# A two-block transformer kernel: the output gate products of the second block placed between the steps of its two attentions

## The chip, the cores and the metric

The kernel runs on one core of a Trainium2 chip, as one program. The metric is the device time of one execution in microseconds (us). The engines are TensorE (PE, with its weight loads as PEld), VectorE (DVE), ScalarE (ACT), GpSimd (POOL) and SyncE (SP), which issues most of the DMAs. Each engine goes through its own list of instructions in order and waits on semaphores.

## What is computed

The input x has 512 tokens of width 1024. A first block (differential attention, sparse attention with compressed keys, merge, MLP) and a second block follow. The change is in the second block, which in the reference is, shortened:

```python
def second_block(x, ...):
    h = x
    # layer 0: FOX
    u = rmsnorm(h, norm_a_g)
    q, k, v, f_logit, gate = split(u @ w_in_a)      # 1024, 1024, 1024, 16, 1024 columns
    q = rmsnorm(q per head); k = rmsnorm(k per head)
    log_f = log_sigmoid(f_logit + b_forget)
    o = fox_attention(q, k, v, log_f)               # 16 heads of 64, causal, with decay c_q - c_k
    h = h + (o * silu(gate)) @ w_out_a
    # layer 1: SWA
    u_kv = rmsnorm(h, kv_norm_g)
    k_s, v_s = split(u_kv @ w_kv)                   # 4 key heads; k normed, partly rotated
    u = rmsnorm(h, norm_b_g)
    q, gate = split(u @ w_in_b)                     # 1024, 1024; q normed, partly rotated
    o = swa_sink_attention(q, k_s, v_s, sinks)      # 16 query heads, window of 128, a sink logit
    h = h + (o * silu(gate)) @ w_out_b
    return h
```

## The kernel before

The program is one list for each engine, built by nested Python functions. All matrix products are made of three passes with numbers split in a high and a low part (high x high, high x low, low x high), in fp32r.

`plan()` gives an ordered table of product groups in runs. A group makes 512 output columns from 1024 rows. Its weights come in units of 512 x 512 numbers (1 MB): SP loads a unit into one of two slots of `RAW` (`weights`, issued at L352), ACT makes the high part in `SPL` (`split_hi`, L488 with a norm gain as scale, L494 without), DVE the low part (`split_lo`, L779 with the gain, L787 without), and PE multiplies (`unit` and `product`, L1421), into four of the eight PSUM banks, alternately for even and odd groups. A unit is split while PE works on the one before. `evict` copies a finished group out of PSUM: into `QKV` (L528), through Silu into `MX` (L532), or onto the residual `X`. Normed groups then go through POOL (squares L1331, rotation L1340) and DVE (`norm_one`, `norm_two`, L828 to L861) with a square root on ACT (L549).

The run `fox_in` has the gate columns first (`fgate0`, `fgate1`: 192 matmuls), then the narrow forget gate `fg`, queries, keys and values; the forget gate's sums over time are made by small chains on DVE (`forget`, `decay_sums`) and stored in DRAM. The run `swa_in` has keys and values (`skv`), queries (`sq0`, `sq1`) and, last, the gate columns (`sgate0`, `sgate1`: 192 matmuls). The attention follows, then the output run (`fox_out`, `swa_out`), for FOX with the next layer's norm behind it.

`attend` is one function for all four attentions. A unit is a pair of heads, there are eight units in FOX and in SWA, and a unit has four steps, one for each tile of 128 queries, from the last tile (t = 3) to the first; in FOX a step has (t+1) x 128 keys, in SWA at most 256. `over_units` runs the first three units and the last three steps written out and those between in a loop with registers. SP copies the unit's query and key columns from `QKV` to a stage (`stage_units`, L371), the values (L386) and in FOX the decays (L379). PE turns queries and keys (`turn`, L1712), ACT and DVE make the high and low parts in `QKT` (L633, L1008). PE makes the scores (`scores_of`: L1649, decays L1655, band L1658, causal mask L1659), DVE the negative maximum (L978, in SWA after it placed the sink, L975), ACT the exponentials with their sums (L614) in `PB`, DVE the reciprocal (L983), POOL scales P (L1369), PE turns P (`turn_p`, L1678), ACT and DVE copy a head each (L625, L1003), and PE makes the values (`values_of`, L1698), for a key tile j at once over all the queries that see it, so 128 to 512 columns, and head 0 and head 1 into different halves of the partitions. In FOX and SWA, DVE then multiplies the output of the unit by the finished gate (L1026), ACT and DVE split the result into `HT` (`high` L638, `low` L1032), which the output product reads. The P of one unit is turned while the scores of the next are made:

```python
if scores: scores_of(m, 3)
if last:   values_of(b.before(), 0)
if values: turn_p(b, 3)
```

`X` (the residual) and `Y` share one region of SBUF; `PB` shares the region of `SPL`, so that weights of the output run can be split only after the attention (`hold=` in `run`). After FOX come the angles for the rotation in SWA (`angles` on DVE, a sine on ACT, L763), before the output run.

## Time and profile before

| | us |
|---|---|
| median of 3 runs | 1947.2 (1944.85 to 1955.84) |
| the profiled execution: its own time | 1947.98 |
| its span from first to last instruction | 1946.2 |
| PE busy | 1759.8 (90%) |
| DVE busy | 892.9 (46%) |
| ACT busy | 705.7 (36%) |
| POOL busy | 366.0 (19%) |

Mean granted TensorE clock over the span: 0.940 of 2.4 GHz. DMA moved 154.85 MB, 80 GB/s in the mean.

How to read it: times are of one execution. A PE matmul's end is modelled, so "busy" says that PE had matmuls under way, not that it was at its peak. The second block lies between about 1294 us and the end: FOX between 1485.8 and 1612.87, SWA between 1786.1 and 1892.67.

### The profile page before, as it was taken

How to read it: one execution, taken by the hardware profiler on the slowest of the kernel's cores; microseconds unless marked ns; L12 is line 12 of the kernel's file. 1: busy time of each engine (PE TensorE's matmuls, PEld its weight loads, DVE VectorE, ACT ScalarE, POOL GpSimd, SP SyncE). 2: the span in 40 equal slices, each digit the busy share in tenths (PEclk: the TensorE clock that was granted, in tenths of full speed). 3: DMA queues.
4: the chain of work that ended last, by engine and by line, in shares of the span. 5: the costliest groups of instructions: out<-in, count | busy, mean ns of one | idle time of the engine just before them, and what ended most of it. 6: DMA issues, size and time to landing. Idle time of an engine off the chain costs nothing.

```text
span 1946.2 us, 24116 instructions
## 1 busy us (share of the span) xinstructions
PE 1759.8 (90%) x8846; PEld 1348.3 (69%) x8846; DVE 892.9 (46%) x1569; ACT 705.7 (36%) x1525; POOL 366.0 (19%) x490
## 2 busy tenths in 40 slices
PE   2999888999978998997999999989998998798878
PEld 2888656887664554886888888868775546686547
DVE  2485274224544665344342234231662653353661
ACT  3322365122135666323341233132323552433550
POOL 4251042102213655010000000000111440020320
PEclk9999797999987999999999999989998998898899
DMA  5223222323102221432223232322222112132211
GB/s 128 85 87 122 73 76 65 108 87 108 44 12 52 58 67 30 153 108 87 66 89 105 88 107 87 108 65 86 87 82 71 55 34 88 64 108 68 63 41 68
DMA packets 148049, 154.85 MB, mean 80 GB/s; under 512 B 48972, under 2 KB 90172, under 8 KB 147960
## 3 DMA queue, kind: packets, MB, share of 16 engines
q1 hardware_dynamic: 141768, 152.74, 24.8%
q0 software_dynamic: 992, 0.86, 0.3%
q10 hardware_dynamic: 5200, 0.02, 0.3%
q8 instruction: 61, 1.00, 0.2%
q14 instruction: 28, 0.23, 0.0%
HBM read 123.15 MB, written 2.15 MB: 64 GB/s over the span
## 4 chain that ended last, share of the span: by engine, by line
PE 83%; DVE 7%; ACT 6%; issue 3%; ACTq 1%; POOL 0%; DVEq 0%; POOLq 0%
PE ps L1421 61%; PE ps L1649 4%; PE ps L1678 3%; PE ps L1698 3%; PE ps L1712 2%; ACT pb L614 2%; PE ps L1659 2%; DVE qkt L1008 1%; ACTq L476 1%; DVE nm L978 1%; ACT qkt L633 1%; PE ps L1655 1%; PE ps L1549 1%; PE ps L1519 1%; PE ps L1620 1%
## 5 line engine op out<-in xcount | busy, mean ns | idle before, releaser
L1421 PE MATMUL ps<-spl,ht 128*128 128x512 f32 x2496 | 583.0, 396 | 31.5 <-DVE spl L787 16.3
L1421 PEld LDWEIGHTS ps<-spl,ht 128*128 128x128 f32 x2496 | 477.8, 192 | 135.0 <-issue 13.6
L787 DVE TENSOR_TENSOR spl<-raw,spl 128x1024 fp32r<-128x1024 f32 x196 | 253.5, 1336 | 568.5 <-ACT spl L494 568.5
L494 ACT ACTIVATE spl<-raw 128x1024 fp32r<-128x1024 f32 x196 | 196.3, 1052 | 640.0 <-PE ps L1421 639.1
L1421 PE MATMUL ps<-ht,spl 128*128 128x512 f32 x1536 | 351.8, 391 | 2.0 <-DVE spl L787 2.0
L1421 PEld LDWEIGHTS ps<-ht,spl 128*128 128x128 f32 x1536 | 289.9, 189 | 63.2 <-issue 2.9
L614 ACT ACTIVATE pb<-ps,nm 128x512 f32<-128x512 f32 (+5 forms) x320 | 161.4, 513 | 85.9 <-DVE nm L978 85.9
L978 DVE TENSOR_REDUCE nm<-ps 128x1 f32<-128x512 f32 (+5 forms) x320 | 140.0, 467 | 81.9 <-PE ps L1659 78.7
L1421 PE MATMUL ps<-spl,uu 128*128 128x512 f32 x768 | 174.4, 389 | 0.0
L1421 PEld LDWEIGHTS ps<-spl,uu 128*128 128x128 f32 x768 | 144.1, 188 | 29.9
L1649 PE MATMUL ps<-qkt 64*128 64x256 f32 (+2 forms) x960 | 126.4, 372 | 15.8 <-issue 7.0
L1331 POOL TENSOR_TENSOR sq<-qkv 128x2048 f32<-128x2048 f32 (+1 forms) x15 | 51.5, 3435 | 451.2 <-ACT qkv L528 436.6
L1678 PEld LDWEIGHTS ps<-idf,pb 128*128 128x128 f32 x672 | 74.9, 144 | 62.4 <-issue 51.2
L1369 POOL TENSOR_TENSOR pb<-pb,rr 128x256 f32<-128x256 f32 (+3 forms) x128 | 81.5, 660 | 191.3 <-DVE rr L983 191.2
L1649 PEld LDWEIGHTS ps<-qkt 64*128 64x128 f32 x960 | 80.0, 208 | 49.5 <-issue 40.8
L1369 POOL TENSOR_TENSOR pb<-pb,rg 128x512 f32<-128x512 f32 (+3 forms) x160 | 112.8, 721 | 7.5
L1698 PE MATMUL ps<-pt,stv 128*64 128x256 f32 (+3 forms) x512 | 94.1, 446 | 20.3 <-ACT pt L625 11.0
L1678 PE MATMUL ps<-idf,pb 128*128 128x128 f32 x672 | 109.9, 289 | 0.0
L625 ACT ACTIVATE pt<-ps 128x256 f32<-128x256 f32 (+3 forms) x160 | 67.8, 424 | 86.5 <-PE ps L1678 86.1
L1008 DVE TENSOR_TENSOR qkt<-ps,qkt 128x512 fp32r<-128x512 f32 x80 | 54.9, 686 | 94.6 <-ACT qkt L633 94.6
L1421 PE MATMUL ps<-ys,spl 128*128 128x512 f32 x384 | 88.9, 394 | 0.0
L1379 POOL MEMSET nws<- 128x2048 f32 x2 | 3.6, 1807 | 440.0 <-PE ps L1421 440.0
(244 smaller groups left out, 1562.8 us busy)
## 6 DMA issues: line engine op xcount, KB each, us to landing
raw<-w_in SPq DMA_DIRECT2D x30, 1024.0 KB, 5.2
raw<-w_mlp_up SPq DMA_DIRECT2D x16, 1024.0 KB, 5.2
raw<-w_mlp_down SPq DMA_DIRECT2D x16, 1024.0 KB, 5.1
raw<-w_in_a SPq DMA_DIRECT2D x16, 1024.0 KB, 5.3
stq<-qkv SPq DMA_DIRECT2D x56, 256.0 KB, 2.7
raw<-w_in_b SPq DMA_DIRECT2D x8, 1024.0 KB, 5.1
stq<-qkv SPq DMA_DIRECT2D x48, 128.0 KB, 2.5
raw<-w_proj_diff SPq DMA_DIRECT2D x4, 1024.0 KB, 5.1
```

The source lines that it names most:

```text
L494: act.activation(SPL[:, n % 2, HI, 2 * k:2 * k + 2], RAW[:, n % 2, 2 * k:2 * k + 2], ACT.Copy).then_inc(hi_done, 1)
L614: last = act.activation(p, PS[:, 2 * (idx % 2) + h, 0:w], ACT.Exp, bias=NM[:, m.slot, h, t:t + 1], accum_out=LS[:, m.slot, h, t:t + 1])
L625: act.activation(PT[odd][:, 0 if a.is_diff else idx % 2, 0:w], PS[:, 4 + odd, 0:w], ACT.Copy)\
L787: dve.tensor_tensor(SPL[:, n % 2, LO, 2 * k:2 * k + 2], RAW[:, n % 2, 2 * k:2 * k + 2], SPL[:, n % 2, HI, 2 * k:2 * k + 2].bitcast(F32), A ...
L978: dve.tensor_reduce(top, bank[:, 0:w + a.sink], AX.X, ALU.max, negate=True).then_inc(s["mx"], 1)
L1008: dve.tensor_tensor(QKT[:, m.slot, i, LO], PS[:, 7], QKT[:, m.slot, i, HI].bitcast(F32), ALU.subtract)\
L1331: pool.tensor_tensor(SQ[:, :, 0:w], QKV[:, :, col:col + w], QKV[:, :, col:col + w], ALU.mult)\
L1369: last = pool.tensor_tensor(p, p, by[:, m.slot, h, t:t + 1].to_broadcast([P, w]), ALU.mult)
L1421: last = pe.matmul(PS[:, b0 + b], left[:, x], right[:, y], start=(kt == 0 and i == 0), stop=(kt == UK * g["units"] - 1 and i == 2))
L1649: pe.matmul(PS[:, 2 * (idx % 2) + h, 0:w], QKT[r, m.slot, 0, x, P * t:P * t + P], QKT[r, m.slot, 1, y, P * a.first_key(t):P * t + P], star ...
L1678: last = pe.transpose(bank[:, P * i:P * i + P], PB[:, m.slot, h, o:o + P], IDF[:])
L1698: last = pe.matmul(PS[HD * h:HD * h + HD, 6, cols], STV[:, m.slot, j, v], PT[h][:, idx % 2, 0:w], start=(idx == 0 and not (a.is_nsa and m. ...
```

## The change

The gate groups leave `fox_in` and `swa_in`. They become a "side" group of eight tiles (128 gate columns each, 24 matmuls), whose weights come in four units of 256 columns x 1024 rows. A tile's 24 matmuls are cut in five pieces (6, 6, 3, 6, 3) that PE does between the steps of a unit of attention. In FOX one tile (`lead=1`) is made before the first scores, in SWA two. The tile is copied raw into `MX` by ACT (`keep_tile`), and Silu comes for all eight tiles at the end of the attention.

The attentions FOX and SWA get a function of their own, `attend_beside`, fully written out (64 steps in all, no loop). Queries, keys and values are read in place from `QKV` (no staging); in SWA keys are turned once for two units. P is kept in three buffers of one step each (`PBS`), in FOX in the region of `X`; so the residual is stored in DRAM during `fox_in` (`XD`) and loaded again after the last P was turned. P is turned one step after its scores, and its values made one step after that; the values are made for each query tile by blocks of 128 x 128. A finished unit's output is copied over its own query columns; the multiplication by the gate and the split (`gated`, `gated_hi`) follow for all eight after the attention. Weights of the side units and of the first two output units are split during the attention, in halves (`side_hi`, `side_lo`), so the output run starts with split weights. The angles move beside the output products. The core of the diff:

```diff
+        [("fq0", ...), ("fg", ...narrow...), ("fq1", ...)] + fk0, fk1, fv0, fv1
+    runs["fox_side"] = [("fgate", "w_in_a_2", FGATE, 0, 4, "side", "ht", ("side",))]
...
-        + [(f"sgate{i}", "w_in_b_2", D + W * i, 0, 2, "col", "ht", ("act", "Silu", "mx", i)) for i in range(2)])
+    runs["swa_side"] = [("sgate", "w_in_b_2", D, 0, 4, "side", "ht", ("side",))]
...
+FOX = Attention("fox", 8, lead=1, run="fox_side")
+SWA = Attention("swa", 8, banded=True, lead=2, run="swa_side")
+EARLY, LATE = 0, 1
+SIDE_KTS = {(0, LATE): (0, 2), (1, EARLY): (2, 4), (1, LATE): (4, 5), (2, EARLY): (5, 7), (2, LATE): (7, 8)}
+PT_BANK, PV_BANK, SIDE_BANK = 0, 2, 3
...
 SP:
+            weights(RUNS["fox_in"], only=4)
+            sp.wait_ge(freed["dve"], RUNS["mlp"][-1]["freed"])
+            sp.dma_start(XD, X[:].rearrange("p t n -> p (t n)")).then_inc(x_parked, 16)
+            weights(RUNS["fox_in"], skip=4)
...
+            side_weights(FOX, 0)
+            sp.wait_ge(cum_out, 16)
+            sp.wait_ge(n_done, RUNS["fox_in"][4]["normed"] + 1)
+            decays(0)
+            decays(1)
+            side_weights(FOX, 1)
+            side_weights(FOX, 2)
+            side_weights(FOX, 3)
+            decays(2)
+            decays(3)
+            weights(RUNS["fox_out"], only=1)
+            decays(4)
+            weights(RUNS["fox_out"], skip=1, only=1)
+            for m in range(5, FOX.units):
+                decays(m)
+            sp.wait_ge(*need(FOX, "pt_tr", FOX.steps))
+            sp.dma_start(X[:].rearrange("p t n -> p (t n)"), XD).then_inc(x_back, 16)
...
 ACT, attend_beside:
+                for n in range(a.steps + 2):
+                    m, i = divmod(n, NT)
+                    if n + 1 < a.steps:
+                        exps(n + 1)
+                    if i == 1 and m:
+                        keep(m - 1)
+                    if i == 0 and m + 1 < a.units and a.new_keys(m + 1):
+                        high(m + 1, 1)
+                    if i == 3 and a.tile_at(m) is not None:
+                        keep_tile(a.tile_at(m))
+                    if 1 <= n <= a.steps:
+                        turned(n - 1)
+                    if n >= a.steps:
+                        silu(2 * (n - a.steps))
+                        silu(2 * (n - a.steps) + 1)
+                    if i == 3 and m + 2 < a.units:
+                        high(m + 2, 0)
+                    if i in (0, 2):
+                        split(m, i // 2)
+                for k in range(4, KT):
+                    silu(k)
...
 DVE, attend_beside:
+                for n in range(a.steps + 1):
+                    m, i = divmod(n, NT)
+                    if n + 1 < a.steps:
+                        maxima(n + 1)
+                    if i == 0 and m + 1 < a.units and a.new_keys(m + 1):
+                        low(m + 1, 1)
+                    if i in (0, 2):
+                        split(m, i // 2)
+                    if n >= 1:
+                        turned(n - 1)
+                    if n + 1 < a.steps:
+                        norms(n + 1)
+                    if i == 3 and m + 2 < a.units:
+                        low(m + 2, 0)
...
 PE, attend_beside:
+                def part(m, i, when):
+                    if a.tile_at(m) is None or (i, when) not in SIDE_KTS:
+                        return
+                    first, end = SIDE_KTS[i, when]
+                    if first == 0:
+                        pe.wait_ge(*need(a, "kept", a.tile_at(m)))
+                        pe.wait_ge(*need(a, "qt", min(m + 2, a.units)))
+                        pe.wait_ge(*need(a, "kt", a.keys_of(min(m + 1, a.units - 1)) + 1))
+                    side(a.tile_at(m), first, end)
...
+                for n in range(a.steps + 2):
+                    m, i = divmod(n, NT)
+                    if n + 1 < a.steps:
+                        scores_of(n + 1)
+                    if n >= 2:
+                        values_of(n - 2)
+                    if i == 0 and m + 1 < a.units and a.new_keys(m + 1):
+                        pe.wait_ge(*need(a, "qt", m + 2))
+                        pe.wait_ge(*need(a, "kept", min(m + a.lead, SIDE_TILES)))
...
+                        turn(m + 1, 1)
+                    part(m, i, EARLY)
+                    if 1 <= n <= a.steps:
+                        turn_p(n - 1)
+                    part(m, i, LATE)
+                    if i == 3 and m + 2 < a.units:
+                        pe.wait_ge(*need(a, "kept", min(m + a.lead + 1, SIDE_TILES)))
+                        turn(m + 2, 0)
```

POOL's `attend_beside` scales the P of a step when its reciprocal is there, as before. `split(m, part)` does half a weight unit in every other unit of attention (units 1, 3, 5, 7 in FOX; 0, 2, 4, 6 in SWA). The lists of ACT and DVE at the end:

```diff
-            attend(FOX)
-            ...sines...
-            run(RUNS["fox_out"], hold=[(A["fox"]["pt_tr"], 4 * FOX.units), (y_lo, 3 * KT)], follow=True, norm=3)
-            run(RUNS["swa_in"], primed=True)
-            attend(SWA)
+            attend_beside(FOX)
+            run(RUNS["fox_out"], primed=True, follow=True, first=lambda: gated_hi(FOX), at={1: sines}, norm=3)
+            run(RUNS["swa_in"], primed=True, follow=True)
+            attend_beside(SWA)
+            run(RUNS["swa_out"], primed=True, first=lambda: gated_hi(SWA))
```

## Rows read from the trace of the kernel before

**Rows 1.** Windows: stage, length, then busy us (count) per engine, granted clock, DMA.
```profile
core 0: us, PE busy (x) PEld busy (x) DVE busy (x) ACT busy (x) POOL busy (x), PEclk, DMA share, GB/s
1485.80:1612.87 127.07, 109.75 (x673) 60.14 (x673) 72.86 (x175) 67.35 (x191) 47.11 (x64) 0.88 0.16 47
1530.00:1542.60 12.60, 12.57 (x88) 6.94 (x84) 8.60 (x20) 7.68 (x24) 6.00 (x8) 1.00 0.22 64
1786.10:1892.67 106.57, 78.55 (x608) 49.65 (x609) 66.16 (x226) 60.29 (x192) 34.41 (x64) 0.88 0.19 45
1838.50:1849.20 10.70, 8.74 (x77) 5.49 (x76) 7.95 (x28) 6.71 (x23) 4.24 (x9) 1.00 0.25 63
```

**Rows 2.** PE's timeline (start, us, what) at the attentions' starts.
```profile
1482.78 0.84 PE L1421 MATMUL ps<-spl,ht 128*128 128x512 f32 x3
...
1742.37 43.68 PE L1421 MATMUL ps<-ht,spl 128*128 128x512 f32 x192
```

**Rows 3.** Windows of PE alone: length, busy us, granted clock, DMA.
```profile
1414.00:1421.00 7.00, 5.28 (x13) 0.52 0.46 150
1503.00:1516.00 13.00, 12.20 (x51) 0.50 0.18 49
1892.67:1899.00 6.33, 6.33 (x16) 0.54 0.64 236
```

**Rows 4.** Waits of PE after 1320 us: us in total, times, longest.
```profile
PE ps L1421 <- DVE cum L1124: 4.3, 1, 4.3
PE ps L1421 <- ACT fl L541: 1.9, 1, 1.9
```

**Rows 5.** Timeline of all engines within a steady FOX unit.
```profile
1532.51 0.96 PE L1649 MATMUL ps<-qkt 64*128 64x512 f32 x6
...
1534.36 1.08 PE L1698 MATMUL ps<-pt,stv 128*64 128x512 f32 x4
...
1535.37 0.44 PE L1678 MATMUL ps<-idf,pb 128*128 128x128 f32 x2
...
1535.96 0.20 ACT L614 ACTIVATION_READ_ACCUMULATOR pb<-ps,nm 128x1 f32 x1
...
1537.36 0.44 PE L1698 MATMUL ps<-pt,stv 128*64 128x128 f32 x4
1537.73 0.66 PE L1678 MATMUL ps<-idf,pb 128*128 128x128 f32 x4
...
1540.17 0.60 ACT L633 ACTIVATE qkt<-ps 128x512 fp32r<-128x512 f32 x1 [0.24 <-PE ps L1712]
...
1540.80 0.69 DVE L1008 TENSOR_TENSOR qkt<-ps,qkt 128x512 fp32r<-128x512 f32 x1 [0.30 <-ACT qkt L633]
```

**Rows 6.** Groups by shape in the two attentions' windows: busy us, mean ns, idle before.
```profile
L494 ACT ACTIVATE spl<-raw 128x1024 fp32r<-128x1024 f32 x3 | 2.9, 1040 | 0.0
L787 DVE TENSOR_TENSOR spl<-raw,spl 128x1024 fp32r<-128x1024 f32 x2 | 2.4, 1222 | 1.4 <-ACT spl L494 1.4
L532 ACT ACTIVATE mx<-ps 128x512 f32<-128x512 f32 x4 | 2.1, 602 | 15.8 <-PE ps L1421 15.8
```

**Rows 7.** Timeline of all engines within a steady SWA unit.
```profile
1837.66 0.62 PE L1649 MATMUL ps<-qkt 64*128 64x256 f32 x6 [0.53 <-DVE qkt L1008]
...
1840.20 0.19 ACT L614 ACTIVATION_READ_ACCUMULATOR pb<-ps,nm 128x1 f32 x1
```

**Rows 8.** Timeline of ACT and DVE beside the products of sq1.
```profile
1723.35 2.03 ACT L528 ACTIVATE qkv<-ps 128x512 f32<-128x512 f32 x4
...
1731.76 2.56 ACT L488 ACTIVATE spl<-raw,lng 128x512 fp32r<-128x512 f32 x4
...
1740.62 0.69 DVE L861 TENSOR_TENSOR qkv<-qkv,sq 128x512 f32<-128x512 f32 x1
```

**Rows 9.** Timeline between FOX's last values and the first output product.
```profile
1606.74 1.28 ACT L763 ACT_TABLE_LOAD   x1
...
1612.87 1.19 PE L1421 MATMUL ps<-spl,ht 128*128 128x512 f32 x2 [7.54 <-DVE spl L787]
```

**Rows 10.** DMA issues: count, KB each, median us to landing.
```profile
x_res<-x SPq DMA_DIRECT2D x1, 2048.0 KB, 7.7
```

More of the change, by code:

```diff
@@ L110, in plan @@
                 tables.append(then[3])
-            out[name].append(dict(by=by, freed=freed[by], name=n, weight=w, col=c, row=r, units=units, kind=kind, src=src, then=then,
+            out[name].append(dict(by=by, freed=freed.get(by), name=n, weight=w, col=c, row=r, units=units, kind=kind, src=src, then=then,
                                   unit=unit, group=group, normed=normed, rotated=rotated, turned=turned,
@@ L151, in __init__ @@
         self.is_diff, self.is_nsa, self.is_fox, self.is_swa = (name == x for x in ("diff", "nsa", "fox", "swa"))
+        self.lead, self.run, self.steps = lead, run, NT * units
     def first_key(self, t):
@@ L318, in program, with score_bank, turn_bank, first_bank @@
         NEXT_GROUP = [RUNS[r][0]["group"] for r in ("diff_in", "mlp", "fox_in", "swa_in")]
+        SIDE = {a.name: RUNS[a.run][0] for a in (FOX, SWA)}
+        TURNS = {a.name: a.turns() for a in (FOX, SWA)}
+        def score_bank(a, s, h):
+            return 4 * (1 - SIDE[a.name]["group"] % 2) + 2 * (s % 2) + h
+        def turn_bank(a, n):
+            return 4 * (SIDE[a.name]["group"] % 2) + n
+        PT_BANK, PV_BANK, SIDE_BANK = 0, 2, 3
+        def first_bank(m, i):
+            return SIDE_BANK if (m, i) not in ((0, 0), (0, 1), (1, 0)) else 2 * m + i
+        def wide(x):
+            return x.rearrange("p k (b n) -> p (k b) n", n=SIDE_W)
+        def kept_output(m):
+            return QKV[:, :, P * m:P * m + P]
+        def by_tile(x):
+            return x.rearrange("p (t n) -> p t n", n=P)
         def reach(eng, s, value):
@@ L342, in weights @@
             def weights(groups, skip=0, only=None):
-                units = [(g, u) for g in groups for u in range(g["units"])][skip:only]
+                units = [(g, u) for g in groups for u in range(g["units"])][skip:][:only]
                 for g, u in units:
@@ L643, in step @@
                         exps(m, 3)
-                    if last and (a.is_fox or a.is_swa):
-                        high(b.before())
                     if values:
@@ L668, in narrow_hi, with gated_hi @@
+            def gated_hi(a):
+                s, base = A[a.name], 2 * KT if a.is_fox else 3 * KT
+                g = SIDE[a.name]
+                act.wait_ge(unit_used, g["unit"] + g["units"])
+                for k in range(KT):
+                    act.wait_ge(*need(a, "gated", k + 1))
+                    act.activation(HT[:, HI, k], MX[:, k], ACT.Copy).then_inc(y_hi, 1)
             def narrow_hi(i, n):
@@ L767, in _, with sines @@
-            attend(SWA)
-            run(RUNS["swa_out"], hold=[(A["swa"]["pt_tr"], 4 * SWA.units), (y_lo, 4 * KT)])
+            run(RUNS["fox_in"], primed=True, follow=True, at={0: lambda: narrow_hi(1, 16), 3: forget})
+            attend_beside(FOX)
+            def sines():
+                act.wait_ge(p_link, N_ANGLE)
+                act.activation(ANG[:, 2], ANG[:, 0], ACT.Sin)
+                act.activation(ANG[:, 3], ANG[:, 1], ACT.Sin).then_inc(small_act, 1)
+            run(RUNS["fox_out"], primed=True, follow=True, first=lambda: gated_hi(FOX), at={1: sines}, norm=3)
@@ L1050, in step @@
                         difference(b, 0)
-                    if last and (a.is_fox or a.is_swa):
-                        low(b.before())
                     if scores:
@@ L1350, in attend @@
                 s = A[a.name]
-                by = RG if a.is_diff or a.is_nsa else RR
                 def unit(m):
@@ L1374, in attend, with attend_beside @@
                     unit(Unit(2 * i + 1, 1, i))
+            def attend_beside(a):
+                s = A[a.name]
+                for n in range(a.steps):
+                    m, i = divmod(n, NT)
+                    t = NT - 1 - i
+                    w = a.width(t)
+                    pool.wait_ge(*need(a, "r", n + 1))
+                    for h in range(2):
+                        p = PBS[a.name][n % 3][:, h, 0:w]
+                        last = pool.tensor_tensor(p, p, RR[:, m % 2, h, t:t + 1].to_broadcast([P, w]), ALU.mult)
+                    last.then_inc(s["scaled"], 1)
             def clear_narrow(last):
@@ L1449, in bank_free @@
                     for o in r:
-                        if o["group"] == g["group"] - 2:
+                        if o["group"] == g["group"] - 2 and o["kind"] != "side":
                             pe.wait_ge(freed[o["by"]], o["freed"])
+                for a in (FOX, SWA):
+                    s, side = A[a.name], SIDE[a.name]["group"]
+                    if g["group"] == side + 1:
+                        pe.wait_ge(*need(a, "e", a.steps))
+                    if g["group"] == side + 2:
+                        pe.wait_ge(*need(a, "pt_a", a.steps))
+                        pe.wait_ge(*need(a, "pt_b", a.steps))
+                        pe.wait_ge(*need(a, "o", a.units))
+                        pe.wait_ge(*need(a, "kept", SIDE_TILES))
             def narrow(g, i):
```

411 lines of the change are left out of this document (314 added, 97 removed).

## Prediction

> **What bounds the kernel now.** I read the windows of the two stages that the change rebuilds, then their timelines, then the waits. The first attention of the second block (FOX) takes 127.07 us, the second (SWA) 106.57 us; a FOX unit of 12.60 us holds 12.57 us of TensorE work, a SWA unit of 10.70 us holds 8.74 us [rows 1]. So the middle of FOX is bound by TensorE, and SWA leaves 2 us free per unit; the rest of the free time lies at the ends. The gate products run as a dense block of 192 matmuls in 43.68 us ahead of SWA, and an equal block ahead of FOX [rows 2]. The stages to compare are, before: FOX from the last projection product (1483.62) to the first output product (1612.87), 129.3 us, plus 43.7 = 173.0; SWA from the end of the query products (1742.4) to 1892.67 = 150.3, its gates included. FOX starts after a pause of TensorE, and the granted clock is then 0.50 (the 1.2 GHz level) until about 1516 [rows 3], over two units. That is the largest thing the change can win.
>
> **The work that moves.** A gate tile is 24 matmuls, 5.46 us [rows 2]; it moves, it doesn't vanish. Value products change their cut. One with 512 columns takes 1.01 us (1534.36 to 1535.37), one with 128 columns 0.37 (1537.36 to 1537.73) [rows 5]: 0.16 fixed and 0.213 per 128 columns. After, each 128x128 block is its own product with its own weight load. I count 0.05 once and 0.32 per block: ten blocks in four groups 3.4 us against 2.77, +0.63 per FOX unit; seven blocks in SWA, +0.33. Bounds: a gain of nothing, and ten times 0.37, +0.93. The Trainium skill (TensorE: Matmul & The Clock Gate, Engine queue depths) says that the queue pulls weight loads ahead of running matmuls; by that the finer cut would be free and the kernel 8 us faster than my sum. The 0.16 fixed part of the rows speaks for the loads being paid. A FOX unit is then 12.57 + 0.63 + 5.46 = 18.7 us of TensorE, a SWA pair with one key turn fewer 28.9 us.
>
> **The waits that the new order adds.** ACT and DVE go through their lists in order. I walk a unit by the code of the diff with the durations of the rows; time 0 is the start of the 512-column scores that stand in a unit's fourth step.
> FOX, fourth step: scores 1.85 (1532.51 to 1534.36), values 1.01, turning P 0.59 (the row's 0.66 less its drain) [rows 5]: TensorE is at the query turn at 3.45. That turn uses the gate tile's bank, and the tile's copy stands in ACT's list behind both exponentials, which end 3.65 after the scores began (1532.51 to 1536.16) [rows 5]. With 0.6 for the copy the turn starts at 4.35: a wait of 0.9. Next unit, first step: scores at 4.95, values, key turn and P turn end at 8.2. The gate piece after them writes the bank from which the keys are split, so it waits for ACT's high part (behind the exponentials, which end at 8.2) and DVE's low part, 0.60 and 0.69 [rows 5]: 9.65, a wait of 1.4. Steps two and three have none. Period 18.7 + 2.3 = 21.0 us.
> In every other unit a weight unit is split in halves, 1.04 us on ACT and 1.22 on DVE [rows 6]. In step three ACT has its half behind its copy of the turned P, DVE has its half ahead of its own copy. Values and the next maxima wait for both: +1.65 us per such unit.
> FOX in all: start 7.4 (three turns and one dense tile, beside which ACT and DVE get ready), unit 0 17.2, six units at 21.0, three splits 5.0, from there to the last P turn 21.0. Then a new tail: copy 0.3, table load 1.28 [rows 9], eight Silu at 0.52 [rows 6], the last output's copy 0.6, high 0.63, low 0.69, in all 8.1. TensorE idles 7.5 us in it, as it does today at that place (7.54) [rows 9]. Sum 184.7 against 173.0: **+11.7**. That the clock stays at 1.00 at FOX's start, dense work leading in, is within this sum.
> SWA, two units: exponentials end 2.73 after the scores began (1837.66 to 1840.39) [rows 7]. By the same walk the query turns wait 1.3 and 1.4, and the key's copies hold the gate piece 1.9. In the even unit the split half of step one holds DVE's copy of P: exponentials 7.35, copy 7.6, high half 1.5, low half 1.6, copy 0.3, so 11.2, and TensorE wants it at 8.2: 3.0. The half of step three costs 2.5. Waits 10.1, pair 39.0 us; two units and two tiles are 32.3 today. The 1.5 lies between 1.28 by elements and 2.56 by count (four instructions of half the width of the 2.56) [rows 8]; most of such a duration goes with the elements in rows 6. The pair that splits output weights, without scale: 37.5.
> SWA's start: the norm of the last query half is no longer hidden by the gate block. For the first half it took 18.0 us from ACT's copy (1723.35) to the last add (1741.31) [rows 8], 2.1 the copy and 14.9 of the rest its own steps. After, ACT first splits a side unit (3.0), so it ends at 20.0. ACT's root waits in it until 11.6, so tile 0 is copied at 14.0 only, and TensorE is idle from 7.5 to 14.1. The clock then falls: after today's last such pause 6.33 us of dense work ran at 0.54 [rows 3], 3 us lost. Scores start at 22.7. Unit 0 12.1, unit 1 20.7, pairs 39.0 and 37.5, two last units 28.0, tail 8.1: 168.1 against 150.3: **+17.8**.
> At nothing: the residual parked in DRAM. Out, some 30 us pass before a weight unit behind it is wanted; back, 23 us of output products run before it is read. 2 MB landed in 7.7 us [rows 10], which is the cost without that cover. The staging copies of Q, K and V vanish, 56 by the code; SP had time for them. The angles move beside output products. The forget gate's two waits, 1.9 and 4.3 us [rows 4], keep their distance. In SP's list the decay loads wait for scores, and the weights behind them are wanted a unit or more later; each staging step it drops stood nowhere on the path.
> Sum: 1947.98 + 11.7 + 17.8 = 1977.5, against the profiled execution (1947.98, span 1946.2), which is 0.8 above the median of 1947.2; **1976.5** on the median. Some 30 waits good to 0.3 us each, and value blocks from -8 to +4, give 1962 to 1992.
> The Trainium skill (ScalarE: Activation LUTs, What ACT_TABLE_LOAD costs) adds a drain of 1.38 us to a switch of tables; by that the two tails are 2.8 us longer. The row shows 1.28 and the next work behind it at once where that was ready, and the sum goes by it.
>
> **Rivals.** **A, TensorE stays the bound** and the waits don't come up. FOX: eight units of 13.2 and eight tiles 149.3, tail 7.5, last chain 3: 159.8, 13 less than today. SWA: four pairs 115.6, the start's pause with its clock 11, last chain 3, tail 7.5: 137.1, 13 less. Steps at the ends that nothing fills give back 7: 1928 (1921 to 1936). For it: a deeper order (P is turned two steps after its scores, three buffers for P), ACT 7.68 and DVE 8.60 of 12.60 us busy [rows 1]. Against it: the waits come from the order in the lists, not from load. It decides if the copies end before TensorE asks, 1.4 us earlier in FOX. 0.18.
> **B, half the waits**, where exponentials end earlier than in my walk. The waits outside start and tail are 16 and 8 us in FOX and 32 in SWA; half is 28, 1948.5 (1941 to 1958). 0.14.
> **C, the clock falls inside SWA.** One pause of 4.3 us [rows 4] put 5.28 us of work to half clock [rows 3], 2.6 us and more. The waits of 3.0 and 2.5 us come eight times; if the clock falls after six of them for 3.5 us, it is 21 more: 1998. Against it: the wait of 1.9 us passed at full clock. 0.07. The Trainium skill (TensorE: Matmul & The Clock Gate, Why this matters for your kernels) warns of idle gaps between bursts; no row here shows one of this size within an attention.
>
> **How the numbers follow.** The main case has 0.61, A 0.18, B 0.14, C 0.07. About 0.5% (9.7 us) is what a measurement of this kernel can tell from no change. The main case and C are slower whole, B is no change but for 0.02 on the slower side, A is faster. So 0.18, 0.12 and 0.70. The range leaves out the lower half of A and the upper half of C: 1930 to 1995; the slower cases alone have 1958 to 1995.
>
> **What would show it.** Right: FOX units near 21 us, SWA pairs near 39; TensorE idle before turns and before the first gate piece of a unit, for copies of ACT and DVE; clock 1.00 at FOX's start; a pause of 6 us in SWA's first 15 us; 7 us idle ahead of each output product. Wrong: FOX units under 19.5 us with TensorE busy over 95%, value blocks at 0.2 us each, or the return of the residual ending a wait.

## The result, and the profile after

The changed kernel takes 2016.8 us in the median of four runs (2014.14 to 2018.71); the kernel before takes 1948.97 beside it. The ratio is 1.0343, with a 95% interval of 1.0309 to 1.0378: 68 us slower. The forecast was 1976.5 with a range of 1930 to 1995: the direction was right, the slowdown more than twice as large as the sum said, and the time outside the range. The profiled execution spans 2017.1 us, 70.9 more than before's, at a mean granted clock of 0.92 (before 0.94).

The two stretches that the prediction compares, in the windows view (length, PE busy, granted clock, DMA share, GB/s), of the changed kernel:

```profile
1443.20:1642.60 199.40, 165.67 (x1058) 0.85 0.08 29
1771.70:1963.90 192.20, 151.06 (x914) 0.78 0.09 30
```

FOX with its gates takes 199.4 us against 173.0 before and 184.7 in the forecast; SWA 192.2 against 150.3 and 168.1. Together they are 68.3 of the 70.9 us. The units answer to [rows 1] (after the length: PE, PEld, DVE, ACT and POOL busy, clock, DMA share, GB/s):

```profile
1520.76:1541.73 20.97, 18.38 (x133) 12.57 (x133) 7.86 (x18) 9.14 (x26) 5.59 (x8) 1.00 0.00 1
1541.73:1565.29 23.56, 19.95 (x133) 13.57 (x133) 8.85 (x21) 8.97 (x25) 5.59 (x8) 0.93 0.13 46
1840.00:1886.90 46.90, 39.51 (x231) 26.47 (x230) 16.74 (x59) 17.39 (x55) 8.61 (x17) 0.75 0.06 23
```

The first is a FOX unit at full clock: 20.97 us, where the walk gave 21.0. The next unit has the same 133 matmuls and takes 2.6 more, at a mean clock of 0.93. The third is a SWA pair, 46.9 us at 0.75, where the walk gave 39.0. So a unit can come out as the walk has it, to a tenth of a microsecond, but most were lengthened by something that the walk left out. The waits of PE (us in total, times, longest), after 1320 us:

```profile
PE ps L2095 <- DVE pts L1309: 26.3, 17, 3.3
PE ps L2119 <- DVE qkt L1314: 15.4, 10, 3.1
PE ps L1713 <- DVE ht L1346: 13.2, 2, 6.6
PE ps L2105 <- ACT mx L810: 11.4, 11, 1.3
PE ps L2119 <- ACT mx L810: 5.1, 1, 5.1
```

L2095 are the values, L2119 the gate pieces, L2105 the turns, L1713 the output products. These are the kinds of wait that the walk has. PE's timeline over one FOX unit and the start of the next, cut to four of the waits, with the same kind of gate piece twice:

```profile
1530.29 1.60 PE L2119 MATMUL ps<-ht,spl 128*128 128x512 f32 x6 [1.65 <-DVE qkt L1314]
1531.83 0.62 PE L2057 MATMUL ps<-qkt 64*128 64x256 f32 x6
...
1544.46 0.88 PE L2095 MATMUL ps<-pts,qkv 128*64 128x128 f32 x12 [0.80 <-DVE pts L1309]
...
1547.06 0.66 PE L2105 MATMUL ps<-idf,qkv 128*128 128x128 f32 x4 [1.14 <-ACT mx L810]
...
1552.36 2.90 PE L2119 MATMUL ps<-ht,spl 128*128 128x512 f32 x6 [1.68 <-DVE qkt L1314]
1555.19 0.82 PE L2057 MATMUL ps<-qkt 64*128 64x256 f32 x6
```

The six matmuls of the gate piece took 1.60 us at 1530.29 and 2.90 at 1552.36. The second time PE had waited 0.80 and 1.14 us shortly before, besides the 1.68 just ahead: the clock had fallen to its lower level (1.2 GHz) after three short pauses and came back after the piece. In SWA's first four units the values wait longer, 2.6 to 2.9 us each time. The cause of one such wait, on DVE:

```profile
1811.17 1.67 DVE L985 SCALAR_TENSOR_TENSOR spl<-raw,lng,spl 128x256 fp32r<-128x256 f32 x4 [5.53 <-ACT spl L579]
1812.76 0.42 DVE L1309 COPY pts<-ps 128x256 f32<-128x256 f32 x1
```

DVE had idled 5.53 us for ACT's high half of a weight unit, whose split stands in its list ahead of the copy of the turned P; PE's values (1813.32) wait for that copy. It is the order in the lists, not load: DVE is busy 36% of the FOX stretch and 41% of SWA's.

### The profile page after: what moved, and what is told of

The parts are those of the page before. It is cut to its first block, busy times and chain, and to the rows that moved or that the text cites. A ratio compares the mean times of both kernels' runs of the same rounds, so it can differ in the third digit from the quotient of the medians.

```text
span 2017.1 us, 24292 instructions
## 1 busy us (share of the span) xinstructions
PE 1803.0 (89%) x9150; PEld 1385.2 (69%) x9150; DVE 892.0 (44%) x1581; ACT 722.0 (36%) x1568; POOL 362.2 (18%) x490
## 3 DMA queue, kind: packets, MB, share of 16 engines
q1 hardware_dynamic: 116584, 145.40, 22.7%
## 4 chain that ended last, share of the span: by engine, by line
PE 79%; ACT 9%; DVE 7%; issue 3%; ACTq 1%; POOL 0%; DVEq 0%; POOLq 0%
PE ps L1713 54%; PE ps L2119 5%; PE ps L1948 2%; PE ps L2095 2%; PE ps L1972 2%; ACT pb L725 2%; PE ps L2077 2%; PE ps L2057 1%; ACTq L568 1%; PE ps L1991 1%; PE ps L2005 1%; DVE qkt L1229 1%; DVE nm L1199 1%; ACT qkt L744 1%; PE ps L1953 1%
## 5 line engine op out<-in xcount | busy, mean ns | idle before, releaser
L1713 PE MATMUL ps<-spl,ht 128*128 128x512 f32 x2496 | 584.3, 397 | 31.8 <-DVE ht L1346 13.2
L1713 PEld LDWEIGHTS ps<-spl,ht 128*128 128x128 f32 x2496 | 478.7, 192 | 135.0 <-issue 13.9
L1010 DVE TENSOR_TENSOR spl<-raw,spl 128x1024 fp32r<-128x1024 f32 x180 | 234.8, 1347 | 524.1 <-ACT spl L605 524.1
L1713 PE MATMUL ps<-ht,spl 128*128 128x512 f32 x1152 | 263.9, 391 | 2.0 <-DVE spl L1010 2.0
L1713 PEld LDWEIGHTS ps<-ht,spl 128*128 128x128 f32 x1152 | 217.6, 189 | 48.1 <-issue 2.9
L1713 PE MATMUL ps<-spl,uu 128*128 128x512 f32 x768 | 174.4, 389 | 0.0
L1713 PEld LDWEIGHTS ps<-spl,uu 128*128 128x128 f32 x768 | 144.2, 188 | 29.9
L2119 PE MATMUL ps<-ht,spl 128*128 128x512 f32 x384 | 122.8, 460 | 20.4 <-DVE qkt L1314 15.4
L725 ACT ACTIVATE pb<-ps,nm 128x512 f32<-128x512 f32 (+1 forms) x192 | 99.8, 530 | 45.7 <-DVE nm L1199 45.6
L1199 DVE TENSOR_REDUCE nm<-ps 128x1 f32<-128x512 f32 (+1 forms) x192 | 85.3, 486 | 54.6 <-PE ps L1953 54.4
L2119 PEld LDWEIGHTS ps<-ht,spl 128*128 128x128 f32 x384 | 77.9, 218 | 41.9 <-issue 22.8
L1713 PE MATMUL ps<-ys,spl 128*128 128x512 f32 x384 | 90.1, 397 | 0.0
L1921 PE MATMUL ps<-idf,xn 128*128 128x128 f32 x128 | 30.8, 421 | 61.2 <-DVE xn L1181 61.2
L1713 PEld LDWEIGHTS ps<-ys,spl 128*128 128x128 f32 x384 | 73.9, 193 | 15.9 <-issue 0.2
L1948 PE MATMUL ps<-qkt 64*128 64x384 f32 (+3 forms) x576 | 77.5, 377 | 7.3 <-DVE qkt L1229 3.0
L2095 PE MATMUL ps<-pts,qkv 128*64 128x128 f32 x544 | 53.5, 329 | 29.2 <-DVE pts L1309 26.3
L1665 POOL TENSOR_TENSOR pbf<-pbf,rr 128x512 f32<-128x512 f32 (+3 forms) x64 | 44.7, 720 | 185.5 <-DVE rr L1303 185.5
L1296 DVE TENSOR_REDUCE nm<-ps 128x1 f32<-128x257 f32 (+5 forms) x128 | 54.5, 439 | 37.5 <-PE ps L2067 34.8
```

The source lines that it names most:

```text
L725: last = act.activation(p, PS[:, 2 * (idx % 2) + h, 0:w], ACT.Exp, bias=NM[:, m.slot, h, t:t + 1], accum_out=LS[:, m.slot, h, t:t + 1])
L1010: dve.tensor_tensor(SPL[:, n % 2, LO, 2 * k:2 * k + 2], RAW[:, n % 2, 2 * k:2 * k + 2], SPL[:, n % 2, HI, 2 * k:2 * k + 2].bitcast(F32), A ...
L1199: dve.tensor_reduce(top, bank[:, 0:w], AX.X, ALU.max, negate=True).then_inc(s["mx"], 1)
L1296: dve.tensor_reduce(NM[:, m % 2, h, t:t + 1], bank[:, 0:w + a.sink], AX.X, ALU.max, negate=True)\
L1665: last = pool.tensor_tensor(p, p, RR[:, m % 2, h, t:t + 1].to_broadcast([P, w]), ALU.mult)
L1713: last = pe.matmul(PS[:, b0 + b], left[:, x], right[:, y], start=(kt == 0 and i == 0), stop=(kt == UK * g["units"] - 1 and i == 2))
```

## The experiments

Each kernel is built from the changed one; the parts are combined as the text says. All but the last version are single timed runs. The kernel before took 1949.88 beside e1 to e5, 1947.1 beside the runs whose label begins with f, 1950.2 beside g1 and g2. In these traces FOX starts between 1436.6 and 1443.4 us, though none of the edits touches what stands ahead of it; a single time can differ by as much without a cause in the edit, so the stretches are the safer comparison.

**DVE copies first.** DVE copies the turned P and takes the reciprocals ahead of its half of a weight split:

```diff
+                    if n >= 1:
+                        turned(n - 1)
+                    if n + 1 < a.steps:
+                        norms(n + 1)
                     if i in (0, 2):
                         split(m, i // 2)
-                    if n >= 1:
-                        turned(n - 1)
-                    if n + 1 < a.steps:
-                        norms(n + 1)
```

> One edit: DVE copies the turned P and makes the reciprocal before its half of a weight split, not after. Theory (order of the lists): the waits of the value products on DVE's copies, 26 us in the trace of the changed kernel (0.8 to 3.4 us each, 14 of them), go down to a few us, and as they are the longest pauses of TensorE the granted clock of the SWA units rises from 0.72 to 0.77 towards 1.00: 2016.8 - 20 - 10 = 1987 us. Rival 1 (the waits cost only their own length): 1997 us, with the clock of the units as it was. Rival 2 (the clock falls for another reason and the waits only move to the next copy): over 2010 us.

Measured: 1997.95 us. PE's waits:

```profile
PE ps L2105 <- ACT mx L810: 19.0, 12, 3.2
PE ps L2119 <- DVE qkt L1314: 14.2, 10, 3.1
...
PE ps L2095 <- ACT pts L791: 10.9, 8, 3.1
```

The 26.3 us for DVE's copy fall to 3.5, but 7.6 come back in the wait for the gate tile's copy on ACT (11.4 to 19.0) and 8.0 in the one for ACT's own copy of P: the next late engine. One wait of a chain taken away gives what the next in the chain leaves. The number is that of rival 1, its picture is not: the waits in the attentions shrank by 8.5 us in all, and the clock did change. In FOX it stayed low (0.84, units of 24.4 us, a stretch of 195.3 us), in SWA it rose from 0.78 to 0.88 and the stretch fell from 192.2 to 174.4.

**All three orders.** In addition ACT copies the gate tile ahead of the exponentials of step four, and the gate pieces start in a unit's second step, where they need not wait for the keys' copies:

```diff
-SIDE_KTS = {(0, LATE): (0, 2), (1, EARLY): (2, 4), (1, LATE): (4, 5), (2, EARLY): (5, 7), (2, LATE): (7, 8)}
+SIDE_KTS = {(1, EARLY): (0, 3), (1, LATE): (3, 4), (2, EARLY): (4, 6), (2, LATE): (6, 8)}
...
+                    if i == 3 and a.tile_at(m) is not None:
+                        keep_tile(a.tile_at(m))
                     if n + 1 < a.steps:
                         exps(n + 1)
```

> The edit of the run before, and two more: ACT copies the finished gate tile before the exponentials of the next step, and the first gate piece of a unit moves from the first step to the second (pieces of 9, 3, 6, 6 matmuls). Theory: beside the 26 us the waits at the query turns (14 us) and at the first gate piece (15 us) go, and the clock stays up: FOX units near 19.0 us, SWA pairs near 32 us, 2016.8 - 55 - 12 = 1950 us. Rival 1 (waits by their length alone): 1962 us. Rival 2 (TensorE's own work has grown by the pieces): FOX units over 20.5 us with TensorE over 97% busy, 1975 us or more.

Measured: 1952.06 us, 65 less than the changed kernel, with every matmul of it. Windows of PE (the two stretches, a FOX unit, a SWA unit with a key turn) and waits:

```profile
1441.30:1603.10 161.80, 145.59 (x1057) 0.97 0.11 36
1732.30:1897.30 165.00, 137.59 (x914) 0.85 0.11 35
1484.72:1503.25 18.53, 18.01 (x134) 1.00 0.19 58
1771.94:1794.00 22.06, 20.56 (x122) 0.77 0.15 49
```

```profile
PE ps L1713 <- DVE ht L1346: 13.4, 2, 6.8
PE ps L2095 <- ACT pts L791: 12.1, 11, 3.1
...
PE ps L2095 <- DVE pts L1309: 7.6, 13, 1.0
```

The six inner FOX units are now 18.5 us each, TensorE busy 97% of them, and FOX is 11.2 us shorter than before the change (161.8 against 173.0). SWA, at 165.0 against 150.3, loses 14.7. Its pair of units takes 37.7 us, not the 32 expected, and its clock is still low (0.85), though between unit 0 and the last two no wait is over 1.2 us. This is PE in the unit of 22.06 us, where the key turn (L2108, L2109) goes over to the low clock:

```profile
1773.83 0.66 PE L2095 MATMUL ps<-pts,qkv 128*64 128x128 f32 x8 [0.94 <-ACT pts L791]
1775.04 0.30 PE L2108 MATMUL ps<-idf,qkv 128*64 128x128 f32 x1 [0.56 <-DVE qkt L1314]
1775.27 0.43 PE L2109 MATMUL ps<-idf,qkv 128*64 128x128 f32 x2
1775.63 0.42 PE L2108 MATMUL ps<-idf,qkv 128*64 128x128 f32 x1
1775.98 0.69 PE L2109 MATMUL ps<-idf,qkv 128*64 128x128 f32 x2
```

Pauses of 0.94 and 0.56 us are the only ones in the nine us ahead of this fall.

**Two of the three.** Without the order on DVE:

> The changed kernel with two of the three list edits: ACT copies the gate tile ahead of the exponentials, and the gate pieces start in a unit's second step; DVE's split stays ahead of its copy of the turned P. If the three edits add up (the first alone gave 19, all three 65): 2016.8 - 46 = 1971. If what counts is how many pauses follow one another, then FOX, with 0.8 us left in every other unit, keeps 1.00 and its units are 18.6 and 19.4 us, and SWA, where DVE's waits of 2.6 us stay, still falls to half clock: FOX as in the run with all three (161.8 us stretch) plus 4 x 0.8, SWA 165 + 8 waits of 2.0 more + clock 6: 1952 + 3 + 22 = 1977. If DVE's order is what brings the clock down, the time is 1985 or more.

Measured: 1976.41 us. The number is that of the second theory, but by two errors that cancel: FOX is 178.1 us, where that theory has 165, and SWA 171.5, where it has 187. In FOX the wait of 0.8 us grew to 2.18 once the others no longer hid it, the units with a split took 20.2 to 22.8 us instead of 19.4, and the clock fell in two of the three. Each of them has this one pause and no other over 0.3 us within 20 us of it, so pauses need not follow one another for the clock to fall:

```profile
1477.21 0.70 PE L2095 MATMUL ps<-pts,qkv 128*64 128x128 f32 x4 [2.18 <-DVE pts L1309]
1477.84 4.21 PE L2119 MATMUL ps<-ht,spl 128*128 128x512 f32 x9
```

The first order alone is worth 19 us, the other two 40, all three 65.

**Pauses filled.** The waits stay, and TensorE does useless work in them. Its products are added into the bank of the unit's output, so this kernel serves for its times alone:

```diff
+                def fill(m, i, where):
+                    if a.tile_at(m) is None:
+                        return
+                    for _ in range(FILL.get((a.name, m % 2, i, where), 0) if m or i == 3 else 0):
+                        pe.matmul(PS[:, turn_bank(a, PV_BANK)], HT[:, HI, 0, 0:P], HT[:, HI, 1], start=False, stop=False,
+                                  skip_group_check=True)
```

> The changed kernel, with matmuls of no use (128 x 512, the residual's first tile by its second, added into the bank of the unit's output, which is therefore wrong) put where TensorE waits in the trace of the changed kernel: FOX 4 before the query turn, 6 before the first gate piece, 3 before the values of step four in the units with a split; SWA 4, 4, and 10 before the values that wait 2.6 us. At 0.23 us each they take about as long as the waits, so that no other engine is served later than before. Theory (the pauses of 0.8 to 2.9 us, coming close together, put TensorE to the 1.2 GHz level, and this costs what my sum lacks): the granted clock is 1.00 in FOX from its second unit on and nearly so in SWA, the stretches at half clock inside the attentions (about 78 us in the changed kernel, in which six gate matmuls took 2.90 instead of 1.60 us) vanish, and the kernel takes 2016.8 - 30 = 1987 us (1980 to 1995), though TensorE does more work. Rival (the order of the lists alone makes the units long, the clock falls with the small matmuls and transposes and not with the pauses): the low stretches stay where they are and the time is 2017 or more.

Measured: 1991.38 us. The windows of PE (FOX and SWA stretch, then one FOX unit with a split) and its timeline in that unit:

```profile
1442.80:1630.90 188.10, 169.58 (x1127) 0.93 0.09 31
1760.80:1937.10 176.30, 150.96 (x1008) 0.92 0.10 33
1532.98:1555.04 22.06, 21.51 (x147) 1.00 0.13 49
```

```profile
1534.71 0.94 PE L2139 MATMUL ps<-ht 128*128 128x512 f32 x3
1535.70 0.88 PE L2096 MATMUL ps<-pts,qkv 128*64 128x128 f32 x12
...
1536.92 1.17 PE L2139 MATMUL ps<-ht 128*128 128x512 f32 x4
1538.30 0.66 PE L2106 MATMUL ps<-idf,qkv 128*128 128x128 f32 x4 [0.21 <-ACT mx L811]
```

L2139 is the fill. FOX's six inner units alternate between 20.97 and 22.06 us, all at 1.00; the same units without the fill took 20.97 to 26.9. A unit without a split at full clock is as long with the fill as without it, so there the fill neither delays nor hastens what TensorE waits for; a unit with a split never stayed at full clock in the changed kernel. More work on the bound engine made the kernel 25 us faster: that is the clock, and the pauses had lowered it. The low clock of the last unit of each attention, where no fill stands, stayed. The rival of the expectation is out: the small matmuls and the turns are the same, and the clock stayed up where the fill stands.

**The changed kernel again.**

> The changed kernel itself once more, beside the same chip's run of the kernel before: 2014 to 2019, with the stretches at half clock inside the attentions at the same places of the program to within a few us if the pauses set them; at other places if something outside the program does.

Measured: 2010.41 us, a little under the range expected. PE's waits are the same to 0.3 us (here the first three rows; in the first execution 26.3, 15.4 and 13.2), but for the one on ACT's copy of P, 3.8 against 2.9:

```profile
PE ps L2095 <- DVE pts L1309: 26.3, 17, 3.3
PE ps L2119 <- DVE qkt L1314: 15.1, 10, 3.1
PE ps L1713 <- DVE ht L1346: 13.4, 2, 6.8
```

But FOX's unit 3, 20.97 us the first time, took 24.36, and a SWA unit of 23.60 us took 20.02. Most low stretches lie at the same places, some do not. So with pauses of this size the clock's fall is not certain from run to run, and SWA took 185.4 us instead of 192.2, FOX 202.8 instead of 199.4. That is 3.5 of the 8.3 us between the two executions (2018.7 and 2010.4); the other 4.9 stood already at FOX's start, in work that is the same in both.

**Gates dense, attention after.** All eight tiles ahead of the first scores, in both attentions (`lead=8`), the weight units split there too:

> All eight gate tiles are made before the first scores (lead 8 in both attentions), nothing between the steps; everything else of the change stays (unrolled, read in place, parked residual, gate after the attention). Theory: it is the placing between the steps that costs. FOX units near 12.8 us and SWA units near 10 us, clock 1.00 in them, one wait of about 0.8 us for the copy of each tile in the dense part; in SWA the dense part covers the last norm. 2016.8 - 35 (FOX) - 50 (SWA) = 1930 us, below the kernel before. Rival (the in-place attention itself is slower: finer value products, silu at the end, parked residual): 1955 us or more, units over 14 and 12 us.

Measured: 1955.76 us. The number is the rival's, its picture is not, for the units are short: 12.9 us in FOX (12.5 before) and 9.6 to 9.9 and 11.9 in SWA (before 10.7 in the mean). What the theory lacked is ahead of them. Each tile's copy held the next tile by 1.0 us (a tile every 6.42 us instead of 5.46), of which 0.69 shows as a wait:

```profile
PE ps L2124 <- ACT mx L806: 14.0, 14, 5.0
```

One of the 14 is SWA's start with 5.0, the others are 0.69 each. The first unit of SWA took 17.3 us. The SWA stretch was 161.7, shorter than the 165.0 with the pieces beside it in their best order. The FOX stretch was 168.1: so 4.9 of the 11.2 us that FOX gains with all three orders come without any weaving, and with the seven holds of a tile taken off (6.7 us) a dense FOX would be at 161.4 by my estimate, level with the 161.8. That FOX gains by the weaving is therefore not shown; no run has a dense FOX with two banks.

**Silu woven into the tail.** The version with all three orders, with the last Silus done between the high parts, so that the first output operand is ready after two Silus and not after eight:

```diff
+                    if k + 2 < KT:
+                        act.activation(MX[:, k + 2], MX[:, k + 2], ACT.Silu).then_inc(s["silu"], 1)
```

> The edits of the second run, and the Silus woven into the splitting of the gated outputs: only two Silus stand before the first output product's operand instead of eight. Theory: the pause before each output product falls from 6.6 us to about 3.5 us: 6 us less than the second run, and less of the output product at 1.2 GHz. Rival (another step sets the start, such as the table load or the last output's copy): the same time as the second run within 2 us.

Measured: 1942.81 us. The pauses before the output products fell from 6.7 to 3.8 us each, and the kernel by 9.3, which is 3.5 more than the pauses. None of that is the output's clock, which over its first 20 us is 0.87 and 0.85 where it was 0.87 and 0.88: 1.8 us stood already at FOX's start, and 1.9 came inside SWA (mean clock 0.88 against 0.85), where nothing was edited.

**SWA's start.** ACT's high parts and its copy of tile 0 stand ahead of the root of the last query half, DVE's low parts ahead of that norm, and a one-column Exp loads the table early:

```diff
                     evict(groups[-1])
+                    if groups is RUNS["swa_in"]:
+                        swa_first()
                     root(groups[-1])
...
+                    act.activation(PBS[a.name][2][:, 0, 0:1], EPSC[:], ACT.Exp)
```

> The version with the three list edits and the woven Silus (1942.8 in its run), and SWA's start mended: ACT makes the high parts of the first turns and copies gate tile 0 ahead of the root of the last query half, DVE makes the low parts ahead of that norm and takes the first maxima between the norm's two halves, and the table of Exp is loaded by a one-column Exp ahead of tile 1's copy. Theory (the start's idle time of 5.05 us, the clock behind it and the table load of 1.28 us are ordering costs): no pause of TensorE before tile 1, its 24 matmuls 5.5 instead of 8.26 us, first scores some 7 us earlier, first maxima 3 us earlier, kernel 1934 (1931 to 1938). Rival (the norm of the last query half on DVE and POOL sets when the first unit runs, wherever its steps stand): first values no earlier, kernel 1941 to 1945.

Measured: 1930.34 us, 12.5 less, somewhat more than the theory said. The wait of 5.05 us for tile 0's copy is 0.7. The SWA stretch, from the last projection product to the first output product, is 151.3 us (1724.39 to 1875.64) after 160.3, so 9 of the 12.5 are the edit's; the rest already stood at FOX's start, and is the difference of one run from another.

**A hybrid.** FOX with the pieces, SWA with dense tiles in two alternating banks, so that no tile waits for a copy:

```diff
-SWA = Attention("swa", 8, banded=True, lead=2, run="swa_side")
+SWA = Attention("swa", 8, banded=True, lead=8, run="swa_side")
...
+        def tile_bank(a, k):
+            return turn_bank(a, PT_BANK if a.lead == 8 and k % 2 else SIDE_BANK)
```

> FOX with the gate pieces beside it, as in the mended version; SWA with all eight gate tiles made ahead of its first scores, alternately in two banks so that TensorE does not wait for a tile's copy, and with the mended start. Theory (in SWA the pieces do not fill TensorE's idle time, since its units are as long as the chain through the engines plus the piece): the SWA stretch falls from 160.3 to 146 to 152 us, kernel 1929 to 1935. Rival (the pieces cover waits that come back when they leave): SWA units of 12 us and more with the clock at half in some, stretch 158 or more, kernel over 1940.

Measured: 1925.95 us. The SWA stretch is 141.8 us (1729.75 to 1871.55), 9.5 less than with the pieces and 8.5 less than before the change: better than the theory's 146. Then the last weight split was taken out of the way of the first maxima, and this version was timed five times:

```diff
-                    if a.lead == 8 and k % 2:
+                    if a.lead == 8 and k in (1, 3, 5):
```

> The hybrid (FOX beside its gate pieces, SWA behind dense gate tiles), with the last output unit's split taken out of the way of SWA's first maxima and into the first unit, half by half, behind the copies of the turned P. Theory (DVE's split of that unit, 2.36 us, and ACT's, 1.99, which stand ahead of the first maxima and exponentials, make the wait of 3.92 us before the second scores, and with it the half clock of 1783 to 1790): that wait falls under 1.5 us, the low stretch goes, the first unit takes 12.5 instead of 14.9 us, kernel 1921 (1919 to 1924). Rival (the chain of the first steps through all engines sets it anyway): 1925 to 1927. Timed in rounds against the kernel before: 1.3% faster, give or take 0.3.

Measured: 1925.39 us (1921.77 to 1931.56, five runs) against 1950.2, ratio 0.9878 (0.9856 to 0.9900). The windows of PE over the eight tiles, SWA's units, and two and a half units in steady state:

```profile
1732.90:1776.00 43.10, 43.10 (x192) 1.00 0.28 98
1775.80:1872.00 96.20, 76.22 (x703) 0.94 0.04 12
1808.90:1835.50 26.60, 23.17 (x227) 1.00 0.01 2
```

The wait of 3.92 us fell to 0.85, but one of 3.50 took its place at the first values (1784.80), where ACT's half of the split now stood ahead of its copy, and the clock fell at the same place. The rival has the number, and the SWA stretch, 142.5 us, is no shorter than the hybrid's 141.8. The version beats before by 1.2% and the changed kernel by 91 us, with the change's FOX in mended order and a SWA whose gate products are one block again.

## Why the prediction was wrong

The prediction's terms beside the changed kernel and the kernel with its pauses filled, in us. A SWA unit is counted from the scores made in the fourth step of the one before.

| | forecast | changed | pauses filled |
|---|---|---|---|
| FOX: start | 7.4 | 6.9 | 6.9 |
| unit 0 | 17.2 | 19.3 | 19.3 |
| six units, splits in | 131.0 | 140.3 | 129.1 |
| last unit and tail | 29.1 | 32.8 | 32.8 |
| sum | 184.7 | 199.4 | 188.1 |
| SWA: start | 22.7 | 22.2 | 22.3 |
| unit 0 | 12.1 | 15.9 | 15.9 |
| unit 1 | 20.7 | 26.2 | 21.4 |
| units 2, 3 | 39.0 | 47.2 | 39.8 |
| units 4, 5 | 37.5 | 38.5 | 39.1 |
| last two and tail | 36.1 | 42.3 | 37.9 |
| sum | 168.1 | 192.2 | 176.4 |

**The step that failed is the clock inside the attentions.** The main case took it at 1.00 but for SWA's start, and rival C put it at 21 us, in SWA alone, with a chance of 0.07. The difference of the last two columns is 11.3 us in FOX and 15.8 in SWA, 27 of the 38.8 us that the sum lacked; with the second execution of the changed kernel in place of the first it is 24. The argument against C was that one wait of 1.9 us had passed at full clock. That row shows one pause in dense work. In the changed kernel the clock fell behind pauses of 0.8 to 2.9 us that stand a few us apart; one pause of 2.18 us by itself did it in two units of three, and 0.94 with 0.56 was enough in SWA. FOX had waits of 0.9 and 1.4 and a delay of 1.65 in my own walk, and I asked of none what they do to the clock. The Trainium skill (TensorE: Matmul & The Clock Gate, A second HAM failure mode: psum-queue depth-cycling) tells of a kernel whose frequent small pauses between groups of matmuls made the clock go up and down. The trace agrees: 1.60 against 2.90 us for the same six matmuls. I had drawn on another section of that page (Why this matters for your kernels), which speaks of gaps between bursts, and set the chance too low.

**The walk of the waits was right.** FOX waits 0.94 at the query turn (forecast 0.9) and 1.65 at the gate piece (1.4), and the six units with pauses filled are within 2 us of the sum. In SWA the values wait 2.6 to 2.9 in the first four units (forecast 2.5 and 3.0), and the pairs with pauses filled are 0.8 and 1.6 us off. SWA's start was right in length (22.2 against 22.7) and in its half clock, with 5.05 us idle where the walk has 6.6.

**Value blocks: wrong, and partly hidden by an opposite error.** I charged 0.63 us per FOX unit for the finer cut. The trace has 1.03 us for four key blocks of both heads (the line at 1465.45 to the next at 1466.48):

```profile
1465.45 1.09 PE L2095 MATMUL ps<-pts,qkv 128*64 128x128 f32 x16
1466.48 1.66 PE L2119 MATMUL ps<-ht,spl 128*128 128x512 f32 x6
1467.97 0.82 PE L2077 MATMUL ps<-idf,pbf 128*128 128x128 f32 x6
```

The four groups of a unit take 1.03, 0.80, 0.59 and 0.37, 2.8 us, against 2.77 before. A block more costs 0.22, and the fixed 0.16 of [rows 5] is paid once in a group, not in part by each block. The Trainium skill's rule (TensorE: Matmul & The Clock Gate, Engine queue depths) is that the queue pulls weight loads ahead, by which the cut would be free; the trace agrees, with 2.8 against 2.77. The other error is that the gate tile keeps its 5.46 us only when dense: its five pieces take 1.54, 1.49, 0.88, 1.50 and 0.86, 6.3 in all, some 0.2 more for each cut. The unit without its two waits is 18.4 (20.97 less 0.94 and 1.65), where I had 18.7; the two errors leave 0.5 us of that unexplained.

**The split's price was wrong in place.** I added 1.65 us to each FOX unit with a split. It cost 1.1 (22.06 against 20.97 with the pauses filled). In the changed kernel it shows as a wait of 0.80 at the values and 0.20 more at the query turn (1.14 against 0.94).

**Ends.** FOX's unit 0 (+2.1) has a pause of 3.11 us for the key's copy, behind a load of the Exp table (1.28 at 1450.86) that my walk does not name, and the gate piece after it took 2.90 us: the clock was not at 1.00 throughout FOX's start, as the sum has it (0.91 over the unit; 0.55 over the first 30 us before). SWA's unit 0 (+3.8) is under-walked: ACT and DVE stand in its split while its first values are wanted, and the load of the Exp table is missing there too. The last units (+3.7, and +1.8 with pauses filled) have a wait for DVE's copy of 3.35 us in FOX and 3.03 in SWA, with the clock at 0.61 over FOX's, which the forecast had as an ordinary unit. For the tables the Trainium skill (ScalarE: Activation LUTs, What ACT_TABLE_LOAD costs) adds a drain to the load; by that each switch would cost 1.38 us more. The trace does not show it:

```profile
1634.85 0.28 ACT L791 ACTIVATE pts<-ps 128x128 f32<-128x128 f32 x1 [1.97 <-PE ps L2077]
1635.14 1.28 ACT L826 ACT_TABLE_LOAD   x1
1636.43 1.15 ACT L826 ACTIVATE mx<-mx 128x512 f32<-128x512 f32 x2
```

ACT's last copy ends at 1635.13, the load follows at once, and the Silu behind it too.

**At nothing, and it was.** The residual was on its way back from 1634.84 for 8.0 us, and no wait ends on it. The dropped staging and the parked copy cost and gave nothing that a wait shows; no run took them apart.

**Rivals.** A failed as the forecast argued: the waits came up. Its FOX was not out of reach: with three edits of order the FOX stretch is 161.8, near its 159.8. Its picture of SWA (137.1) was not reached by any version with pieces: the best has 151.3, and the one with dense tiles 141.8. B, half the waits, did not occur. C had the right cause, but only in SWA.

**The arithmetic.** 1977.5 less the 0.8 is 1976.7, not 1976.5; it changes nothing.

What stays open is what exactly makes the clock fall: the same waits gave a full-clock unit once and a slow one the next time. The remaining 11.7 us between the filled kernel and the forecast are the terms named above, read from one run.

## What to carry to other kernels

When work is woven between the steps of an attention, walk the lists as done here, but then price the pauses in the walk for the clock as well: here 62 us of waits in the attentions cost 24 to 27 more by the clock of TensorE. Put the copies that TensorE waits for ahead of weight splits and exponentials in the lists of the other engines; here two such edits, and the gate pieces begun a step later, gave back 65 of 68 us. Make the dense version too before crediting the weaving. In the stage that waits for the chain through the engines (SWA) one dense block was 9.5 us better than the best woven version. It ran at a clock of 1.00 and stood over the norm of the last queries; no run takes the two apart. In FOX the woven version (161.8 us against 173.0) beat the dense one that was run (168.1), but by the estimate above it would not beat one without the waits for copies.

## What the runs showed of the hardware that was not expected

- Useless matmuls in TensorE's pauses made the kernel 25 us faster (2016.8 to 1991.4): the granted clock over the FOX stretch rose from 0.85 to 0.93 and over SWA's from 0.78 to 0.92.
- Two executions of one program, with all but one of the waits equal to 0.3 us, had the clock fall in different units (FOX unit 3: 20.97 and 24.36 us); both attentions together took 391.6 and 388.2.
- The clock fell behind pauses of 0.94 and 0.56 us in one unit (at 1775.6, all three orders), while a unit with pauses of 0.94 and 1.65 us stayed at 1.00 (at 1520.8, changed kernel).
- A group of value products pays a fixed part of about 0.16 us once, however finely it is cut (1.03, 0.80, 0.59 and 0.37 us for four to one blocks); a gate tile cut in five pieces costs 0.8 us more than in one (6.3 against 5.46).
